# Finishing each stage of a two-layer trunk in token halves, with the norm between stages woven into its last tiles

## The reference

```python
def rmsnorm(x, g):
    y = x * lax.rsqrt(jnp.mean(x * x, axis=-1, keepdims=True) + EPS)
    return y * g

for layer in range(2):
    x = x + (even_mixer, odd_mixer)[layer](rmsnorm(x, g_mix[layer]), ...)
    x = x + conv_ffn(rmsnorm(x, ffn_norm[layer]), ...)
```

## Time and profile before

| | us |
|---|---|
| median of 3 runs | 2264.36 (2261.55 to 2266.15) |
| the profiled execution, its time | 2261.34 |
| the same, first to last instruction (span) | 2259.3 |
| TensorE busy in it | 2128.4 |
| VectorE, ScalarE, GpSimd busy | 1289.8, 946.8, 1103.4 |
| mean granted TensorE clock | 0.971 |

### The profile page before, as it was taken

One profiled execution on the slowest core, in us unless ns is written; L12 is line 12 of the kernel. 1 busy time (PEld: TensorE's weight loads), 2 busy tenths in 40 slices (PEclk: granted clock), 3 DMA queues, 4 the chain that ended last, 5 costly groups with the idle time before them and its releaser, 6 DMA issues. The chain is left out here.

```text
span 2259.3 us, 29928 instructions
## 1 busy us (share of the span) xinstructions
PE 2128.4 (94%) x11534; PEld 1031.6 (46%) x11534; DVE 1289.8 (57%) x1969; ACT 946.8 (42%) x1391; POOL 1103.4 (49%) x765
## 2 busy tenths in 40 slices
PE   6989967889899999999999999799999999999998
PEld 3544435644344444444444444465444444444444
DVE  9788888846764156415644032885866217631752
ACT  6459856634552055205323221743464115411520
POOL 5104324215884567466585032312697457745732
PEclk8999989999999999999999999899899999999999
DMA  4001100002122112211241011102112212221112
GB/s 168 20 10 47 34 26 1 13 18 62 38 65 66 50 44 56 73 41 55 61 117 51 0 34 28 43 6 59 40 38 56 66 46 56 56 66 47 56 42 89
DMA packets 186214, 109.87 MB, mean 49 GB/s; under 512 B 4095, under 2 KB 180646, under 8 KB 186102
## 3 DMA queue, kind: packets, MB, share of 16 engines
q1 hardware_dynamic: 185638, 107.00, 16.3%
q0 software_dynamic: 464, 1.39, 0.2%
HBM read 104.18 MB, written 4.19 MB: 48 GB/s over the span
## 5 line engine op out<-in xcount | busy, mean ns | idle before, releaser
L637 POOL TENSOR_SCALAR w_scaled<-stage 128x1024 f32<-128x1024 f32 (+4 forms) x114 | 115.1, 1010 | 791.5 <-PE ps L913 494.9
L992 PE MATMUL ps<-h_hi,arena 128*128 128x512 f16 x1280 | 391.3, 381 | 10.8 <-DVE arena L2403 6.5
L913 PE MATMUL ps<-arena,w_hi 128*128 128x512 f16 x1408 | 366.2, 383 | 15.9 <-DVE xT L2288 6.3
L992 PE MATMUL ps<-arena 128*128 128x512 f16 x1440 | 317.3, 379 | 0.1
L2359 DVE SCALAR_TENSOR_TENSOR xT<-ps,xT 128x1024 f32 (+1 forms) x64 | 78.3, 1223 | 339.3 <-PE ps L913 290.4
L992 PE MATMUL ps<-h_lo,arena 128*128 128x512 f16 x640 | 243.8, 381 | 0.0
L2412 DVE SCALAR_TENSOR_TENSOR work<-ps,fvec,work 128x1023 f32<-128x1023 f32 (+1 forms) x176 | 221.4, 1279 | 25.5 <-ACT work L1677 22.4
L913 PEld LDWEIGHTS ps<-arena,w_hi 128*128 128x128 f16 x1408 | 138.3, 99 | 186.9 <-issue 8.8
L992 PEld LDWEIGHTS ps<-arena 128*128 128x128 f16 x1440 | 140.8, 98 | 170.2 <-POOL arena L713 0.6
L913 PE MATMUL ps<-arena,w_lo 128*128 128x512 f16 x704 | 211.7, 383 | 0.0
L992 PEld LDWEIGHTS ps<-h_hi,arena 128*128 128x128 f16 x1280 | 125.7, 98 | 165.4 <-issue 14.8
(11 more groups left out here) (373 smaller groups left out, 3788.5 us busy)
## 6 DMA issues: line engine op xcount, KB each, us to landing
stage<-in_ffn_w_up_dram SPq DMA_DIRECT2D x76, 512.0 KB, 4.6
stage<-in_ffn_w_down_dram SPq DMA_DIRECT2D x32, 512.0 KB, 4.2
stage<-in_od_w_in_dram SPq DMA_DIRECT2D x20, 512.0 KB, 3.7
stage<-in_ev_w_in_dram SPq DMA_DIRECT2D x12, 512.0 KB, 3.7
arena<-in_ffn_w_up_dram SPq DMA_DIRECT2D x12, 512.0 KB, 4.8
stage<-in_ffn_w_down_dram SPq DMA_DIRECT2D x16, 384.0 KB, 3.4
arena<-in_x_dram SPq DMA_DIRECT2D x8, 512.0 KB, 7.2
out_dram<-arena SPq DMA_DIRECT2D x8, 512.0 KB, 4.7
```

Of the source, the lines that this page charges most:

```text
L637: nc.gpsimd.tensor_scalar(scaled, src, W_SCALE, 1.0, ALU.mult, ALU.mult).then_inc(w_parts, 1)
L913: last = mm(out2[:, hf * HALF:(hf + 1) * HALF], w, a[:, k0 + k, hf * HALF:(hf + 1) * HALF], start=(first and k == 0 and pss == 0), stop=(l ...
L992: last = mm(ps[:, bank, :], left, right[:, k, :], start=(fresh and k == 0 and pss == 0), stop=(k == 3 and pss == 2), skip_group_check=True)
```

## The change

- The last two tiles (6 and 7) of each of the four stage ends are made by token halves: first half of 6, first half of 7, second half of 6, second half of 7 (`tail_units`). Adds and squares of these are halves too (`add_tile_half`, `square_half`, `add_square_half`).
- All eight squares are now summed in `ssq` by VectorE; TensorE sums each half of the tokens with four single-column matmuls (`norm_sums`) in place of eight and eight.
- The diagonal is gone: TensorE transposes a repeated column of `rms8` (`spread`, `tr`), four times for a half.
- For the first token half the sums and the spread stand within the last two tail units; for the second half they stand within `first_two_units`, behind k = 2 and k = 5 of its first half.
- The tail's weights have their own tiles (`tail_hi`, `tail_lo`), so GpSimd splits them, and the next stage's first two units, without waiting for TensorE to free `w_hi` and `w_lo`. In `WOVEN`, "down" 7, "r" 0 and "r" 1 come earlier; "tm" 6's high part goes from ScalarE to GpSimd, and GpSimd's low parts of norm 2 go to VectorE.
- ScalarE makes the high part of the raw weights of the ffn's second feature tile (`first_raw_high`) behind tiles 5 and 6 of the norm, where it was ahead of tile 0; GpSimd's `su_low_raw(layer, 1)` moves between the two halves of its low parts. ScalarE's scaling of the next weights (`scale_second`) is cut in two, behind tiles 9 and 11.
- At the end 8 of the 16 groups of transposes stand within the last two tail units, and the stores of the first four token blocks can start there.

```diff
-POOL_NORMS = (1, 2, 3)
+POOL_NORMS = (1, 3)
...
-                 ("down", 5), ("tm", 4), ("down", 6), ("tm", 5), ("down", 7), ("tm", 6), ("r", 0), ("tm", 7), ("r", 1)]
-
-        TM_HIGH_BY_ACT = (1, 2, 3, 4, 5, 6)
+                 ("down", 5), ("tm", 4), ("down", 6), ("down", 7), ("tm", 5), ("r", 0), ("r", 1), ("tm", 6), ("tm", 7)]
+
+        TM_HIGH_BY_ACT = (1, 2, 3, 4, 5)
...
+            def spread(n, hf):
+                pe.wait_ge(rstd_ready, 2 * n + hf if n else 1)
+                for j in range(4):
+                    b = 4 * hf + j
+                    last = tr(ps[:, 7 - hf, j * P:(j + 1) * P], rms8[:, b:b + 1].broadcast_to([P, P]), ident[:])
+                last.then_inc(rstd_spread, 1)
+
+            def norm_sums(n, hf):
+
+                blocks = range(4 * hf, 4 * hf + 4)
+                pe.wait_ge(sq_added, sq_base(n) + 8 + 2 * hf)
+                for b in blocks:
+                    last = mm(ps[:, 6, b:b + 1], ssq[:, b * P:(b + 1) * P], ones[:, 0:1], start=True, stop=True)
                 last.then_inc(ssq_summed, 1)
...
+            def tail_units(base, nk, weights, hi, lo, k0, pairs, split_at, between):
+
+                for hf in range(2):
                     for mi in range(2):
+                        if hf == 0:
+                            pe.wait_ge(x_added, 2 + base + 5 + mi)
+                            pe.wait_ge(w_split, split_at[mi])
+                        for k in range(nk):
+                            wh, wl = (w[mi][:, k * P:(k + 1) * P] for w in weights)
+                            for pss, (w, a) in enumerate(((wh, hi), (wh, lo), (wl, hi))):
+                                last = mm(half_of(pair(pairs[mi]), hf), w, a[:, k0 + k, hf * HALF:(hf + 1) * HALF],
+                                          start=(k == 0 and pss == 0), stop=(k == nk - 1 and pss == 2))
+                            if k == nk - 1:
+                                last.then_inc(unit_done, 1)
+                            if (hf, mi, k) in between:
+                                between[hf, mi, k]()
...
+                    elif g == 2:
+                        tail_units(DOWN_AT[layer, g], nf, [[w[:, mi, :] for mi in range(2)] for w in (w_hi, w_lo)], hid_hi, hid_lo, 0,
+                                   (p0, p0 + 1), [ready + 6 + mi for mi in range(2)],
+                                   {(1, 0, 2): lambda: turns_out(0, 4), (1, 1, 1): lambda: turns_out(4, 8)})
+                        turns_out(8, 16)
...
+            tail_units(EV_AT, KT - EARLY_KS, (tail_hi, tail_lo), mix_hi, mix_lo, EARLY_KS, (0, 1),
+                       [unit0["ev_out"] + 7 + mi for mi in range(2)],
+                       {(1, 0, 3): lambda: norm_sums(1, 0), (1, 1, 1): lambda: spread(1, 0)})
```

More of the change, by code:

```diff
@@ L88, with build @@
 NVEC = _n
[L91 to L94 removed]
+POOL_NORMS = (1, 3)
+def build(nc, t, out):
     ctx = ExitStack()
@@ L227, in build @@
         r01, r23 = view(10752, [2, T]), view(21536, [2, T])
+        tail_hi, tail_lo = ([view(10752 + 768 * part + 384 * mi, [6 * P], F16) for mi in range(2)] for part in range(2))
+        out_tok = view(8192, [NB, D])
         w_gate = view(12800, [GH * DK])
@@ new lines, in turns_out @@
+            def turns_out(t0, t1):
+                for t in range(t0, t1):
+                    b, g = TURNS_OUT[t]
+                    if t in (0, 12):
+                        pe.wait_ge(x_added, 2 + X_ALL - (2 if t == 0 else 0))
+                    if 4 <= t < 12:
+                        pe.wait_ge((out_act, out_dve)[t % 2], (t - 4) // 2 + 1)
+                    for j in range(4):
+                        k = 4 * g + j
+                        last = tr(ps[:, 4 + t % 4 if t < 12 else t - 12, j * P:(j + 1) * P], xT[:, k, b * P:(b + 1) * P], ident[:])
+                    last.then_inc(out_turned, 1)
@@ new lines, in root, with norm @@
+            def root(n, hf):
+                act.wait_ge(ssq_summed, 2 * (n - 1) + hf + 1)
+                A(rms8[:, 4 * hf:4 * hf + 4], ps[:, 6, 4 * hf:4 * hf + 4], ACT.Sqrt, bias=eps[:, 0:1], scale=1.0 / D).then_inc(rms_ready, 1)
+            def norm(n, base):
+                square_half(n, base, 0, 0)
+                square_half(n, base, 0, 1)
+                root(n, 0)
+                square_half(n, base, 1, 0)
+                for m in range(2 * KT):
+                    high(n, m)
+                    if m == 3:
+                        square_half(n, base, 1, 1)
+                    if m == 5:
+                        root(n, 1)
+                    if n % 2 and m in (5, 6):
+                        first_raw_high(n // 2, m - 5)
+                    if n % 2 and m in (9, 11):
+                        scale_second(n // 2, (m - 9) // 2)
@@ L2360, in add_tile @@
                                            op0=ALU.mult, op1=ALU.add).then_inc(x_added, 1)
-                with dve.Fori(0, 4 if n is None else 3) as i:
+                with dve.Fori(0, 4 if whole else 3) as i:
                     for mi in range(2):
@@ L2454, in ffn @@
                     hidden_low(f0 + nf - 1)
[L2455 removed]
+                    residual(f"down{layer}{'abc'[g]}", 2 if g == 2 and layer == 0 else None, 2 * bank_set(f0 + nf - 2), whole=g < 2)
             def odd():
[L2458 removed]
+                last_pair = 2 * bank_set(FT - 2)
+                norm(2, VEC_AT["od_norm"], "down0c", (last_pair, last_pair + 1))
                 def tm(b, par, b1):
```

416 lines of the change are left out of this document (214 added, 202 removed).

## The result

The changed kernel takes 2252.3 us (median of 5 runs, 2250.2 to 2256.2), the kernel before 2264.7 beside it: ratio 0.995, 95% interval 0.9939 to 0.9961. So 10 to 12 us are gained, and the forecast was 2251.7. The profiled execution took 2250.22 us, its span is 2248.5.

A forecast was written before the change was run, and what follows sets the result against it. TensorE is busy 2128.4 us, and VectorE's four sums set the time in both ffns. Terms 4.5 + 2.0 + 4.5 + 1.4 + 0.3 = 12.7 us off the 2264.36 median give 2251.7; eight in ten: 2243 to 2261.

The forecast's parts named there:

- Norm 1: Norm before the first ffn: VectorE's four sums come 3.0 to 7.4 us earlier against the tail's start, taken as 4.5.
- Norm 3: Norm before the second ffn: VectorE's four sums come 2.0 to 8.2 us earlier, taken as 4.5.
- Norm 2: Norm before the odd mixer: `first_two_units` ends earlier, gain 1.2 to 5.3 us, -1 if TensorE's clock falls; taken as 2.0.
- The new wait: Last two units of the first down-projection: TensorE waits 5.0 us for tile 5's add, behind ScalarE's "tm" 5 high part.
- with all holds: Norm 2's low case, with VectorE operations held beside GpSimd ones: gain 1.2 us.
- The end: Kernel's end: last copy 1.5 us earlier, stores' tail stays at 6.6; gain 0.5 to 2.5, taken as 1.4.
- The start: Kernel's start: without the diagonal VectorE's next work can start 0.6 us earlier; gain 0 to 0.6, taken as 0.3.
- More than forecast: Rival: VectorE's half sums fall between GpSimd's instructions, tile 5's add isn't missed; 20.5 us gained, 2244; chance 0.22.
- The sums gain nothing: Rival: GpSimd's and ScalarE's moved norm work sets the ffn's chain; 0 to 1.5 us per ffn, about 2260; chance 0.17.
- Slower by holds: Rival: GpSimd holds VectorE at every low part in the norms; 4.9 us slower, 2269, deciding from five holds; chance 0.05.
- the two forecast places: TensorE's waits behind norm 1, at 604 and 613 us before the change, said to grow 3 to 4 us in all.
- The rule: Two-SBUF-input VectorE and GpSimd instructions exclude each other for a whole instruction; worst ends stand, sum about 7 us, 2257.

The follow-up runs named there:

- raw_low_last: The changed kernel with GpSimd's `su_low_raw` behind all low parts of the norm instead of between its halves; ratio 0.9938 to the kernel before.
- pool_waits: The kernel both with GpSimd held back at the last of its raw sums until VectorE's four sums are done; ratio 0.9949 to the kernel before.
- spread_only: The kernel before with only the spread by TensorE transposes, in all four norms, without VectorE's diagonals; ratio 0.9998 to the kernel before.
- square_first: The changed kernel with ScalarE squaring tile 4 ahead of "tm" 5's high part before norm 2; ratio 0.9936 to the kernel before.
- both: The changed kernel with the edits of square_first and raw_low_last together; ratio 0.9919 to the kernel before.
- pe_delay: The changed kernel with 16 idle products (3.45 us) on TensorE behind the first two units in each ffn; ratio 0.9933 to the kernel before.

## Why the prediction was right, point by point

- **Norm 1** (4.5): 4.3 to 4.6 in the table, at the forecast places (+9.6, +13.1, +38.75), and all of it reaches the first cross sum. The spread alone gave 0.9 to 1.4; by subtraction the rest is the halves' and what goes with them (own tiles for the tail's weights, the moved splits), which no run took apart.
- **Norm 3** (4.5): 4.9 and 3.2; the smaller one had a spell at 1.2 GHz (granted clock 0.94 and 0.90 in the stretches from 1568 to 1590). The first product came at +12.4, between the forecast's 11.1 and 13.9: both half sums were held, but by 0.5 us each (1.25 and 1.16 for 0.69), not by a whole GpSimd operation, and TensorE waited 1.60 for the second.
- **Norm 2** (2.0): 0.2 to 0.6. The new wait was forecast to 0.2 us, and the first product came at +22.2 to +22.6, past the forecast's +20.2 to +21.9. The step that went wrong here is the price of what follows the wait, put at up to 1.1 of waits and 1.4 of work: three waits for the first half's tiles and the second sums (0.73, 0.99, 0.95 in the second profile) together 2.7, and the column sums and transposes within the stage (1.05 and 0.60). The end "with all holds", 1.2, was still too high.
- **The end** (1.4): 2.8 to 3.0. The last copy came 1.7 earlier (forecast 1.5); the stores' tail, said to stay at 6.6, fell to 5.4. The eight stores are issued over 13.2 us now, before over 7.7, and the median one lands in 3.3 instead of 4.7 us (4.4 in the second profile of before).
- **The start** (0.3): about 2. The diagonal's removal was seen, but not that VectorE's next two instructions stand at another place relative to GpSimd's and take 2.98 instead of 4.83.
- **The sum**: these terms, mean over the two profiles, are 4.5, 4.1, 0.4, 2.9 and 2.3, together 14.2 against 12.7. The measured gain was 10.0 to 12.4. By the means of the two profiles the span shrank by 11.0, nearly these terms less 4.1 lost in the odd mixer and plus 1.1 gained in the even one. In both mixers, which the change doesn't touch up to their last units, the spells at 1.2 GHz fall at other places from one execution to the next; the prediction hadn't them in its sum. The total is nearer than its terms: low terms at start and end, a high one at norm 2 and a loss not thought of cancelled.
- **The rivals.** More than forecast: no, the chain behind the high part was there. The sums gain nothing: no, 4.3 to 4.6 of the norm arrive. Slower by holds: two held low parts in the norm and the last pair, not five. Waits behind norm 3, where no spell fell, grew from 4.98 to 8.54 us, and behind norm 1 by 1.7, with 1.7 more in the unit at 1.2 GHz: 3.4 to 3.6, forecast 3 to 4. They stand ahead of the two forecast places, mostly for GpSimd, and not at them.
- **The rule.** The holds are there: VectorE operations with two SBUF inputs beside GpSimd take 1.16 for 0.69, 2.21 for 0.69, 12.86 for 9.37, while the half adds that read PSUM and one SBUF tile stay at 0.68 and the one-input reduction left GpSimd at its own speed. The Trainium skill (SBUF — State Buffer, SBUF: two separate sides) says that the shared ports are locked for a whole instruction, by a VectorE operation with two SBUF inputs only against a GpSimd one that reads SBUF, and the traces agree: the low part that starts at 538.91 beside a GpSimd instruction ends 0.55 us behind the end of that instruction. The worst ends that the prediction priced with it (2257) didn't come, since few of the moved operations met a GpSimd one. And raw_low_last and pool_waits moved holds without a gain.

Open: what decides in which stretch a spell at 1.2 GHz falls. It differs between executions of one program and seems to lean with the program (spread_only, twice of two). The Trainium skill (TensorE: Matmul & The Clock Gate, Part 1) says of a kernel's first matmuls that the number of slow ones varies from run to run; these traces show such a variation far behind the start, 108.6 and 103.8 us for one stretch of the changed kernel. Open too: whether VectorE's sums or GpSimd's own steps set the start of an ffn, and why the medians of square_first, raw_low_last and both lie lower than their chains explain.

## What to carry to other kernels

Price a reordering at the instruction whose start the next stage hangs on, and then ask what the earlier work will run beside: a gain of 4.4 us at norm 2's first product became 0.7 to 1.0 because it met GpSimd's splits. A VectorE operation with two SBUF inputs and a GpSimd one held each other wherever they met here; moving one moved the hold, so count them over the whole stage. For differences of a few us, compare the distances between fixed instructions in two profiles of each kernel: medians of kernels with the same chain differed by 3 us here, and 4 us of gain in spread_only's chain left no trace in its time.

## What the hardware showed that was not expected

- Work that nobody needs cost nothing: with 6.9 us of it on TensorE pe_delay ran at 0.9933, the changed kernel at 0.995 and 0.9956.
- A spell at 1.2 GHz costs 0 to 4.8 us by its place: nothing in a wait, 1.7 in a dense stretch, 4.8 in the odd mixer's chain of short pieces.
- Spreading four roots over 512 columns by transposes takes TensorE 0.60 us; in the kernel before two products with ones and their diagonals cost 3.10 us from the reciprocal to the first product, with transposes 1.23.
